# Attention keys projected once: two dense key tiles in place of four, with the other half of each tile made by products with the identity

## The reference

```
q, k, v = split(h @ w_qkv, [1024, 1280])         # 16 query heads, 4 key heads, 4 value heads of 64
q = rms_norm(q.reshape(b, L, 16, 64), q_g)
k = rms_norm(k.reshape(b, L, 4, 64), k_g)
...                                              # prompt: attend to k, v; return k and v
qs = apply_axial_rope(qs, rope)                  # sample tokens only
k_lat = apply_axial_rope(k_lat, rope)
k_all = concatenate([k_lat, cache_k]); v_all = concatenate([v_lat, cache_v])
ys = block_attention(qs, k_all, v_all) @ w_out
```

## Time and profile before

| | |
|---|---|
| median of 3 runs | 2429.6 us (2429.53 to 2431.59) |
| the profiled execution: its own time | 2431.41 us |
| the profiled execution: span from first to last instruction | 2429.6 us |
| TensorE granted clock, mean | 0.977 |
| PE busy | 2288.0 us, 94% of the span |
| DVE, ACT, POOL busy | 60%, 35%, 7% |

### The profile page before, as it was taken

One profiled execution on the slowest core, in us unless ns is written; L12 is line 12 of the kernel. 1 busy time (PEld: TensorE's weight loads), 2 busy tenths in 40 slices (PEclk: granted clock), 3 DMA queues, 4 the chain that ended last, 5 costly groups with the idle time before them and its releaser, 6 DMA issues.

```text
span 2429.6 us, 35465 instructions
## 1 busy us (share of the span) xinstructions
PE 2288.0 (94%) x14713; PEld 2020.0 (83%) x14713; DVE 1460.3 (60%) x2194; ACT 839.6 (35%) x1601; POOL 177.0 (7%) x217
## 2 busy tenths in 40 slices
PE   5989889989999998999999999999998999999998
PEld 3868868889888887789999999798555799999997
DVE  4357482357334868667565556789676675555644
ACT  4355372211122135343222223533555442222222
POOL 0000000024101420120000000200000100000002
PEclk9989999999999999999999999999899999999999
DMA  7411205520352012222222212122000022222221
GB/s 293 171 36 52 84 1 204 183 95 1 112 200 79 10 70 78 87 71 87 68 89 74 75 61 87 50 79 70 5 1 1 27 88 61 87 79 63 95 70 44
DMA packets 43854, 193.60 MB, mean 80 GB/s; under 512 B 5008, under 2 KB 5008, under 8 KB 36912
## 3 DMA queue, kind: packets, MB, share of 16 engines
q1 hardware_dynamic: 41472, 178.10, 21.8%
q0 software_dynamic: 2224, 13.24, 1.5%
HBM read 183.72 MB, written 7.60 MB: 79 GB/s over the span
## 4 chain that ended last, share of the span: by engine, by line
PE 83%; DVE 10%; ACT 3%; issue 2%; DMA 1%; SPq 0%; POOL 0%; DVEq 0%; ACTq 0%
PE pg L873 30%; PE pg L912 16%; PE pg L663 16%; PE ps L818 5%; PE ps L1092 2%; PE pg L1072 2%; PE ps L637 2%; PE pg L1047 1%; PE ps L759 1%; PE ps L1047 1%; DMA ring<-in_wstream 1%; DVE rtb L1589 1%; PE ps L778 1%; DVE wlo L1563 1%; PE ps L781 1%
## 5 line engine op out<-in xcount | busy, mean ns | idle before, releaser
L873 PE MATMUL pg<-hh,xhi 128*128 128x320 f32 (+2 forms) x1008 | 314.9, 312 | 6.5 <-DVE hl L1677 6.5
L873 PE MATMUL pg<-hl,xhi 128*128 128x320 f32 (+2 forms) x1008 | 311.5, 309 | 0.0
L873 PE MATMUL pg<-hh,xlo 128*128 128x320 f32 (+2 forms) x1008 | 311.5, 309 | 0.0
L1563 DVE TENSOR_TENSOR wlo<-ring,whi 128x1024 fp32r<-128x1024 f32 x129 | 157.0, 1222 | 188.5 <-ACT whi L1135 188.3
L663 PE MATMUL pg<-hh,whi 128*128 128x320 f32 x976 | 239.8, 327 | 23.6 <-DVE hl L1595 10.4
L663 PE MATMUL pg<-hl,whi 128*128 128x320 f32 x976 | 225.9, 313 | 0.0
L663 PE MATMUL pg<-hh,wlo 128*128 128x320 f32 x976 | 225.8, 313 | 0.0
L663 PEld LDWEIGHTS pg<-hh,whi 128*128 128x128 f32 x976 | 166.1, 192 | 62.4 <-issue 51.6
L873 PE MATMUL pg<-hh,whi 128*128 128x320 f32 (+2 forms) x672 | 209.7, 312 | 3.3 <-DVE hl L1677 3.3
L873 PE MATMUL pg<-hl,whi 128*128 128x320 f32 (+2 forms) x672 | 207.6, 309 | 0.0
L873 PE MATMUL pg<-hh,wlo 128*128 128x320 f32 (+2 forms) x672 | 207.6, 309 | 0.0
(11 more groups left out here) (327 smaller groups left out, 4613.8 us busy)
## 6 DMA issues: line engine op xcount, KB each, us to landing
ring<-in_wstream SPq DMA_DIRECT2D x231, 512.0 KB, 3.7
adaring<-in_wada SPq DMA_DIRECT2D x21, 1024.0 KB, 4.9
ybuf<-in_wada SPq DMA_DIRECT2D x21, 1024.0 KB, 4.9
adabig<-in_wada SPq DMA_DIRECT2D x6, 1024.0 KB, 18.5
xk<-in_x SPq DMA_DIRECT2D x1, 2560.0 KB, 10.8
yssd_scratch<-ybuf POOLq DMA_DIRECT2D x2, 1280.0 KB, 5.8
xk<-yssd_scratch POOLq DMA_DIRECT2D x1, 2560.0 KB, 10.4
xk<-in_x_tok POOLq DMA_DIRECT2D x1, 2560.0 KB, 8.8
```

Of the source, the lines that this page charges most:

```text
L873: last = nc.tensor.matmul(out, w[:, k * P:(k + 1) * P], h[:, k, a:b], start=k == 0 and m == 0, stop=k == KT - 1 and m == 2)
L1563: V.tensor_tensor(lo, flat(ring[:, s % RING]), hi.bitcast(F32), ALU.subtract).then_inc(wlo_ready, 1)
```

## The change

The four key tiles become two, each with two different key heads (0 and 1, 2 and 3), as the weight matrix has them. They move to the front of the stage, before the query tiles, and take buffers `ak[:, 0]` and `ak[:, 2]`. After norm and rotation, steps 4 to 7 make the doubled form from them: in each of these steps PE multiplies 320 tokens of a finished key tile with columns 64 to 127 of the identity (into PSUM partitions 0 to 63) and with columns 0 to 63 (into 64 to 127), so the halves come out exchanged. ACT then writes three quarters: the exchanged lower half to `ak[0:64, k+1]`, a copy of `ak[64:128, k]` to `ak[64:128, k+1]`, and, behind a wait for itself, the exchanged upper half over `ak[64:128, k]`. Two semaphores, `ks_ready` and `ks_done`, order the two engines.

For every head tile, DVE's two products (with `rb`, with the gain) become one `scalar_tensor_tensor`, and the wait between them goes; a wait for `qk_norm` of the tile before, which DVE itself has signalled, is added ahead of the reciprocal.

The stage has 12 steps in place of 14, and the weight stream two slots fewer. The core of the diff:

```diff
+    for i in range(2):
+        full("ak", i)
     for i in range(8):
         full("aq", i)
-    for i in range(4):
-        full("ak", i)
...
+K_TILES = KV_HEADS * HD // P
+N_HEAD_TILES = K_TILES + ATTN_HEADS * HD // P
+NORMS = [8] + [1] * 8 + [8] + [1] * N_HEAD_TILES
...
+        def head_tile(j):
+            return ak[:, 2 * j, 0:NT] if j < K_TILES else aq[:, j - K_TILES]
+
+        def key_swap(r):
+            return 2 * (r // 2), slice(r % 2 * HALF, (r % 2 + 1) * HALF)
...   PE, at the end of step i
+                if 4 <= i < 4 + 2 * K_TILES:
+                    r = i - 4
+                    k, toks = key_swap(r)
+                    pe.wait_ge(rope_done, r // 2 + 1)
+                    if r:
+                        pe.wait_ge(ks_done, r)
+                    for a in range(2):
+                        last = nc.tensor.matmul(ps[HD * a:HD * (a + 1), 0, 0:HALF], cm[:, IDENT, HD * (1 - a):HD * (2 - a)],
+                                                ak[:, k, toks], start=True, stop=True)
+                    last.then_inc(ks_ready, 1)
+            pe.wait_ge(rope_done, N_HEAD_TILES)
+            pe.wait_ge(ks_done, 2 * K_TILES)
...   ACT, at the end of step i
+                if 4 <= i < 4 + 2 * K_TILES:
+                    k, toks = key_swap(i - 4)
+                    act.wait_ge(ks_ready, i - 3)
+                    nc.scalar.copy(ak[0:HD, k + 1, toks], ps[0:HD, 0, 0:HALF])
+                    link(nc.scalar.copy(ak[HD:P, k + 1, toks], ak[HD:P, k, toks]))
+                    nc.scalar.copy(ak[HD:P, k, toks], ps[HD:P, 0, 0:HALF]).then_inc(ks_done, 1)
...   DVE
             def qk_finish(j):
+                buf = head_tile(j)
+                if j:
+                    dve.wait_ge(qk_norm, j)
                 recip(N_QK + j)
-                link(V.tensor_tensor(buf, buf, rb[:], ALU.mult))
-                V.tensor_scalar(buf, buf, par("q_g") if j < 8 else par("k_g"), None, ALU.mult).then_inc(qk_norm, 1)
+                V.scalar_tensor_tensor(out=buf, in0=buf, scalar=par("k_g" if j < K_TILES else "q_g"), in1=rb[:],
+                                       op0=ALU.mult, op1=ALU.mult).then_inc(qk_norm, 1)
...   host
         if kind == "ak":
-            k = w_qkv[:, D_MODEL + HD * i:D_MODEL + HD * (i + 1)]
-            return np.concatenate([k, k], axis=1)
+            return col(w_qkv, D_MODEL + P * i)
```

More of the change, by code:

```diff
@@ L192, in ada_steps @@
     return []
-NORMS = [8] + [1] * 8 + [8] + [1] * 12
+K_TILES = KV_HEADS * HD // P
+N_HEAD_TILES = K_TILES + ATTN_HEADS * HD // P
+NORMS = [8] + [1] * 8 + [8] + [1] * N_HEAD_TILES
 N_ADALN0, N_HG, N_SSD, N_QK = 0, 1, 9, 10
@@ L495, in hybrid_step @@
         rot_ready = sem("rot_ready")
+        ks_ready = sem("ks_ready")
+        ks_done = sem("ks_done")
         rope_done = sem("rope_done")
@@ L1010, in _ @@
             stage("ffn0")
-            t = FIRST_OF["aq"]
-            for i in range(14 + 2):
+            t = FIRST_OF["ak"]
+            for i in range(N_HEAD_TILES + 2):
                 if i == 0:
                     open_stage(t, 1)
-                elif 2 <= i < 14:
+                elif i >= 2:
                     both(t + i)
-                if 1 <= i <= 12:
+                if 1 <= i <= N_HEAD_TILES:
                     norm(N_QK + i - 1, BD64)
-                if 2 <= i <= 13:
+                if i >= 2:
                     j = i - 2
@@ L1024, in _ @@
                         pe.wait_ge(rope_done, j)
-                    src = aq[:, j, 0:SAMPLE] if j < 8 else ak[:, j - 8, 0:SAMPLE]
-                    nc.tensor.matmul(ps[:, 1, :], cm[:, ROT, :], src, start=True, stop=True).then_inc(rot_ready, 1)
-            pe.wait_ge(rope_done, 12)
+                    nc.tensor.matmul(ps[:, 1, :], cm[:, ROT, :], head_tile(j)[:, 0:SAMPLE],
+                                     start=True, stop=True).then_inc(rot_ready, 1)
+                if 4 <= i < 4 + 2 * K_TILES:
[10 more added lines that the diff above has]
+            pe.wait_ge(ks_done, 2 * K_TILES)
             for i in range(2):
@@ L1491, in _ @@
             stage("ffn0")
-            t0 = FIRST_OF["aq"]
-            for i in range(14):
+            t0 = FIRST_OF["ak"]
+            for i in range(N_HEAD_TILES + 2):
                 t = t0 + i
                 preps(t)
-                if i < 12:
-                    dst = aq[:, i] if i < 8 else ak[:, i - 8, 0:NT]
+                if i < N_HEAD_TILES:
+                    dst = head_tile(i)
                     evac(t, dst)
@@ L1500, in _ @@
                 else:
-                    evac(t, wk[:, 2 + i - 12, 0:NT])
-                if 1 <= i <= 12:
+                    evac(t, wk[:, 2 + i - N_HEAD_TILES, 0:NT])
+                if 1 <= i <= N_HEAD_TILES:
                     root(N_QK + i - 1)
+                if 4 <= i < 4 + 2 * K_TILES:
[4 more added lines that the diff above has]
+                    nc.scalar.copy(ak[HD:P, k, toks], ps[HD:P, 0, 0:HALF]).then_inc(ks_done, 1)
             for i in range(2):
@@ L2072, in _ @@
             stage("ffn0")
-            t0 = FIRST_OF["aq"]
+            t0 = FIRST_OF["ak"]
             def qk_finish(j):
-                buf = aq[:, j] if j < 8 else ak[:, j - 8, 0:NT]
+                buf = head_tile(j)
+                if j:
+                    dve.wait_ge(qk_norm, j)
                 recip(N_QK + j)
-                link(V.tensor_tensor(buf, buf, rb[:], ALU.mult))
-                V.tensor_scalar(buf, buf, par("q_g") if j < 8 else par("k_g"), None, ALU.mult).then_inc(qk_norm, 1)
+                V.scalar_tensor_tensor(out=buf, in0=buf, scalar=par("k_g" if j < K_TILES else "q_g"), in1=rb[:],
+                                       op0=ALU.mult, op1=ALU.mult).then_inc(qk_norm, 1)
             def rope_apply(j):
-                buf = aq[:, j, 0:SAMPLE] if j < 8 else ak[:, j - 8, 0:SAMPLE]
+                buf = head_tile(j)[:, 0:SAMPLE]
                 dve.wait_ge(rot_ready, j + 1)
@@ L2226, in _ @@
             gated(1)
-            pool.wait_ge(tile_ready, FIRST_OF["aq"])
+            pool.wait_ge(tile_ready, FIRST_OF["ak"])
             pool.wait_ge(yg_ready, 4 * TT)
```

## The result

The median fell from 2429.62 to 2415.48 us (2411.37 to 2415.87 in four runs), 14.1 us less, where 14.8 were forecast and 2414.8 us stood as the number. The ratio of the runs is 0.9935 with a 95% interval of 0.9922 to 0.9948 (the two medians alone give 0.9942). The profiled execution took 2415.87 us with a span of 2414.1.

The account below looks back on a forecast made before the run. PE was taken to bound the stage's steps. Two steps removed (-17.94), four swaps (+3.4) and the fused instruction (-0.3) gave -14.8 us, so a median of 2414.8 us, range 2411.0 to 2418.5.

Parts of the forecast that it names:

- PE sets the pace, and a step is worth 8.97 us: In the stage's uniform middle, PE is busy throughout each step; removing two steps of 8.97 us saves 17.94 us.
- The swap at 0.85 us, from attention's narrow products: On PE, four added swaps, each 0.54 us for side-by-side halves plus 0.31 for changes of form, add 3.4 us.
- ACT's copies and the waits at nothing: In the swap steps, ACT's three copies (1.3 us) and PE's waits fit into ACT's idle time and cost zero.
- The fused instruction at nothing in the steps and 0.3 at the end: On DVE, 0.42 us gained per step buys nothing under PE's cover; at the stage's end it saves 0.3 us.
- Attention the same: Attention, behind the stage, should take the same time as before; otherwise the prediction is wrong.
- The clock rival: At the stage's end, a 0.3 us shorter stop lets PE's clock hold: 5.2 us more gain, 2409.6 us (chance 0.08).

Follow-up runs that it names:

- e11: The kernel before with only DVE's two products fused into one instruction, profiled at full clock: 111.27 us from the first norm's products to PE's resuming, against 111.54.
- e5: The changed kernel without the swaps (PE's products and ACT's copies left out, attention on wrong keys): 2412.26 us, ratio 0.9926 to the kernel before.
- e3: The changed kernel with each swap's pair of products issued twice: 2413.39 us, ratio 0.9938 to the kernel before.
- e4: The changed kernel with each swap as one full-width product with a ninth constant matrix: 2412.06 us, ratio 0.993 to the kernel before.
- e2: The changed kernel with DVE's two products and the wait between them as they were before: 2413.35 us, ratio 0.9937 to the kernel before.
- e9: The changed kernel itself run once more, beside the kernel before on the same chip: 2415.57 us, ratio 0.9936 to the kernel before.
- e6: The changed kernel with four products on constants filling PE's wait for the last rotation: 2410.62 us, ratio 0.9919 to the kernel before.
- e8: The paired heads of e7 with the four filling products of e6 in PE's wait: 2409.28 us, ratio 0.9916 to the kernel before.
- e7: The changed kernel with heads paired by host ordering, without swaps, doubled keys and four transposes: 2408.67 us, ratio 0.9912 to the kernel before.
- e10: The paired heads of e7 once more, on the same chip as e9: 2409.26 us, ratio 0.9913 to the kernel before.

## Why the prediction was right

*PE sets the pace, and a step is worth 8.97 us.* Right. Plain steps stayed 8.97 to 8.98 us apart in every trace at full clock. From the table, 111.54 - 96.86 = 14.68 us, and each term of it was measured by a run of its own: 17.96 for two steps (e11 against e5), less 3.55 for the swaps (e5 against the change), plus 0.27 at the end (e11 against before).

*The swap at 0.85 us, from attention's narrow products.* Right; 0.88, of which e3 shows 0.54 for both halves and e4 0.34 for the changes of form, where 0.31 had been read from the earlier trace rows. That rows of another place, with 128 columns and other data, priced 320 columns to 4% is the best step of the sum, but the closeness is in part luck. Piece by piece the forecast had 0.15 ahead of the first pair, 0.05 between the pairs and 0.11 behind; the runs show 0.09, 0.05 and 0.19. The 0.15 was a reading too high: the earlier trace rows give only the start of a group of four, and the trace of before has the last of the four at

```profile
1731.79 0.27 PE L1072 MATMUL pg<-cm,rtb 128*128 128x128 f32 x1
```

so that 1731.99 - 1731.79 - 0.11 = 0.09 was lost there too. Against it stands the way back, 0.08 dearer here, where dense products follow.

*ACT's copies and the waits at nothing.* Right; e5 removed them and gained only PE's share. How long ACT would stand was misread (2 us; it was 0.57), which changed nothing, since the cover was 5 us.

*The fused instruction at nothing in the steps and 0.3 at the end.* Right: 0.27 from before (e11) and 0.28 against the change (e2). Its own price was over-estimated: 0.92 from the earlier trace rows, 0.80 here. In the FFN the program has a wait between the two instructions of those rows; here the next one, at 1618.96, starts before the fused one's 0.89 us are over. DVE's idle time grew to 0.84 and not to 0.7. It had no effect on the sum, since ACT's rounding capped the gain.

*Attention the same.* Not quite, and here the sum was incomplete rather than wrong. In the profiled executions the span fell by 15.5 us and A by 14.68. The rest is what no term stood for: B gained 0.27 more (in e9 it did not), attention took 0.7 longer, the part behind it 1.2 less. Over the traces, attention takes 172.9 to 175.5 us and the part behind it 545.1 to 548.1, whatever the kernel, and the stage began between 1583.3 and 1586.6. The change's own four runs spread as widely, 2411.37 to 2415.87. So the stage's 14.7 us against 14.8 are a confirmation, while the whole's falling within a microsecond of 2414.8 is in part luck.

*The clock rival.* It did not happen, and its premise, a stop shorter by 0.3 us, was wrong. The number in brackets is PE's idle time between its last rotation and its resuming, before and in the change:

```profile
1697.19 1.33 PE L707 MATMUL ps<-cm,wk 128*128 128x128 f32 x5 [3.01 <-DVE ak L2088]
1682.51 0.33 PE L719 MATMUL ps<-cm,wk 128*128 128x128 f32 x1 [3.19 <-DVE aq L2119]
```

Before, PE had already stood 0.55 us ahead of that rotation; with the fused instruction it starts the rotation without a wait and then stands 3.19 us in one piece (3.19 in e9 and e11 too, 3.01 in e2). The clock fell as before (0.56 from 1682 to 1689). The rival's price, 5.2 us, is about what e6 measured against e9, 2415.57 - 2410.62 = 4.9, though on different chips; that the gain is a steady one was not shown, and e8 speaks against it.

Attention is short in e2, e6, e7 and e10 and long in the others, and this goes with the clock. With attention as one window, the mean granted clock is 0.95 where it took 174.5 to 175.5 us (before, the change, e3, e4, e8), 0.96 at 175.0 to 175.1 (e5, e9, e11), 0.97 at 173.3 and 173.4 (e7, e10), and 0.98 at 172.9 and 173.0 (e2, e6). What stays open is why the clock falls for longer in the one execution than in the other: apart from the filled wait no run set these instants, and e8, with the wait filled, has 0.95.

## What to carry to other kernels

Where one engine was busy for the whole of a repeated step, a removed step was worth its length to a hundredth of a microsecond, and so was an added instruction on that engine; on the engine beside it half a microsecond a step was worth nothing. Price a new form of instruction from the nearest place where the kernel already uses it, and look there at the distance between the starts of single instructions, at the changes of form in front and behind too. And before paying to bring data into the shape that a consumer wants, ask whether the order of the weights can give the consumer that shape for free: ordering the heads on the host was worth 4.5 us more than the exchange on the chip, 3.55 in the stage and the rest in the transposes ahead of attention (B of e10 and e9).

## What the runs showed of the hardware that was not expected

Two products to opposite halves of PSUM's partitions run side by side also when they read the same moving data: 0.54 us for the second round of both halves, each of 320 fp32 columns (e3).

Holding PE's clock through one stop does not hold it through the next: with the wait filled the clock stayed at 1.00 until 1684 in e8, and then was at 0.50 from 1688 to 1700, after 4 us in which PE was busy for 1.81. The Trainium skill (TensorE: Matmul & The Clock Gate, section What's actually happening) says that the instant of a change varies from run to run. The traces agree: one and the same kernel, the change and e9, has a granted clock of 0.61 in the first 15 us of attention in one profiled execution and 0.73 in the other.
